# Second attention with block transposes on VectorE, a round trip of the probabilities through DRAM, and modulation accumulated in PSUM

## The reference, cut to what matters

```python
def diff_attend(q, k, v, lam):
    s = jnp.einsum('bqhcd,bkhcd->bchqk', q, k).astype(jnp.float32) * (ATT_HEAD_DIM ** -0.5)
    p = jax.nn.softmax(s, axis=-1)
    a = p[:, 0] - lam * p[:, 1]
    return jnp.einsum('bhqk,bkhe->bqhe', a.astype(v.dtype), v)
...
    for l in range(DEPTH_2):
        mod_l = [m[:, None, :] for m in jnp.split(c_act @ ada_w[l] + ada_b[l], N_MOD, axis=-1)]
        mod_c = jnp.split(cc_act @ ada_w[l] + ada_b[l], N_MOD, axis=-1)
```

## Time and profile before

| | us |
|---|---|
| median of 3 runs | 3024.77 (3024.72 to 3024.81) |
| span of the profiled execution | 3023.4 |
| what lies around the span (median less span) | 1.4 |
| second attention of la = 0, first scores to first work behind the barrier | 865.61 to 1009.97: 144.4 |
| second attention of la = 1, the same | 2259.71 to 2331.57: 71.9 |

### The profile page before, as it was taken

One profiled execution on the slowest core, in us unless ns is written; L12 is line 12 of the kernel. 1 busy time (PEld: TensorE's weight loads), 2 busy tenths in 40 slices (PEclk: granted clock), 3 DMA queues, 4 the chain that ended last, 5 costly groups with the idle time before them and its releaser, 6 DMA issues.

```text
span 3023.4 us, 38857 instructions
## 1 busy us (share of the span) xinstructions
PE 2960.7 (98%) x15464; PEld 2267.7 (75%) x15464; DVE 1376.5 (46%) x2609; ACT 802.6 (27%) x1751; POOL 869.7 (29%) x772
## 2 busy tenths in 40 slices
PE   8999999999999999999999999999998999999999
PEld 7776799998855545555558788888886666678998
DVE  1243267812265736555543533342236555541651
ACT  1022222201022325555620110110104355540210
POOL 0000234574400101221234334443230111110786
PEclk9999999999999999999999999999999999999999
DMA  7455434442345132223212122222331323234443
GB/s 258 151 202 210 147 140 164 157 168 84 126 181 221 44 112 99 84 98 108 88 70 84 70 84 86 96 84 84 112 112 42 116 102 112 105 112 153 154 168 112
DMA packets 65561, 370.18 MB, mean 122 GB/s; under 512 B 6298, under 2 KB 21722, under 8 KB 23152
## 3 DMA queue, kind: packets, MB, share of 16 engines
q1 hardware_dynamic: 49120, 334.60, 30.6%
q10 hardware_dynamic: 15296, 29.56, 2.9%
q0 software_dynamic: 976, 3.63, 0.3%
HBM read 362.30 MB, written 1.28 MB: 120 GB/s over the span
## 4 chain that ended last, share of the span: by engine, by line
PE 89%; DVE 6%; PEld 2%; ACT 1%; issue 1%; PEldq 0%; POOL 0%; DMA 0%; POOLq 0%; SPq 0%; DVEq 0%; ACTq 0%
PE PB L482 15%; PE PB L1361 13%; PE PA L482 11%; PE PS L482 8%; PE PB L362 8%; PE PB L1342 6%; PE PB L1076 5%; PE PB L1192 4%; PE PB L1375 3%; PE PB L406 2%; PE PA L1444 2%; PE PA L1413 1%; PE PA L1427 1%; DVE work L2607 1%; PE PB L1245 1%
## 5 line engine op out<-in xcount | busy, mean ns | idle before, releaser
L1361 PE MATMUL PB<-H,ring 128*128 128x512 f32 (+1 forms) x1024 | 428.1, 566 | 0.0
L1361 PEld LDWEIGHTS PB<-H,ring 128*128 128x128 f32 x1024 | 192.0, 190 | 184.4 <-issue 179.0
L517 POOL TENSOR_TENSOR sums<-ring 128x512 f32<-128x512 f32 x115 | 151.0, 1313 | 617.5 <-PE PA L482 247.5
L482 PE MATMUL PB<-work,sums 128*128 128x128 f32 (+1 forms) x1360 | 230.6, 327 | 0.0
L482 PEld LDWEIGHTS PB<-work,sums 128*128 128x128 f32 x1360 | 207.1, 191 | 17.4
L2861 POOL TENSOR_TENSOR work<-work 128x256 f32<-128x256 f32 x96 | 59.7, 642 | 519.0 <-ACT work L1867 417.0
L482 PE MATMUL PA<-work,sums 128*128 128x128 f32 (+1 forms) x1280 | 208.9, 318 | 0.0
L482 PEld LDWEIGHTS PA<-work,sums 128*128 128x128 f32 x1280 | 187.5, 191 | 13.5
L2521 DVE SCALAR_TENSOR_TENSOR work<-PB,par,work 128x510 f32<-128x510 f32 (+3 forms) x256 | 181.7, 713 | 24.1 <-ACT work L1845 17.3
L626 DVE TENSOR_TENSOR work<-PA,work 128x128 f32<-128x128 f32 (+1 forms) x53 | 18.9, 357 | 379.9 <-ACT work L610 379.9
L1342 PE MATMUL PB<-H,ring 128*128 128x512 f32 (+1 forms) x512 | 175.5, 493 | 0.0
(11 more groups left out here) (394 smaller groups left out, 5305.1 us busy)
## 6 DMA issues: line engine op xcount, KB each, us to landing
ring<-stream SPq DMA_DIRECT2D x314, 1024.0 KB, 4.8
sums<-cs_rows ACTq DMA_DIRECT2D x16, 1024.0 KB, 4.7
sums<-cs_rows ACTq DMA_DIRECT2D x16, 512.0 KB, 3.8
work<-work ACTq DMA_DIRECT2D x16, 256.0 KB, 4.5
work<-scratch POOLq DMA_DIRECT2D x1, 2560.0 KB, 13.5
X<-xT SPq DMA_DIRECT2D x2, 512.0 KB, 5.5
ring<-stream SPq DMA_DIRECT2D x2, 512.0 KB, 6.8
X<-xT SPq DMA_DIRECT2D x1, 1024.0 KB, 20.0
```

Source lines behind the costliest of these rows:

```text
L482: mm = pe.matmul(fast_bank(side, bank)[:, col:col + width], weight(k), right(4 * part + k), start=first and opens and k == 0, stop=last an ...
L517: nc.gpsimd.tensor_tensor(su[:, 0], a21, a22, ALU.add).then_inc(sem("w_summed"), 1)
L1361: mm = pe.matmul(PB[:, pair, t, 0:Tc], ring[:, c % SLOTS, k, t * P:(t + 1) * P], H[:, k, 0:Tc], start=(k == 0), stop=(k == KT - 1))
```

## The change

- `turn2` and `turned2` are gone. In their place DVE's 32 x 32 block transpose (`flip2`, L2487) writes the turned blocks of two units (the two query tiles of one head) into one of three buffers AT_F. SP stores that pair to DRAM (`store_turned`, one DMA of 128 rows, 4 KB each for 512 keys and 2 KB for 256) and fetches it back (`fetch_turned`, four DMAs of 32 partitions, runs of 1 KB or 512 bytes), which puts the 32-row groups where the full transpose wants them, into one of four buffers AT_T.
- `values2(n)` now takes a pair of units, with 256 queries as the moving side, and writes PA[0] only. It stands at step 2n + 7 of the loop (`BEHIND` = 6): one transfer round trip behind. `out2` copies a pair at once.
- The modulation chunks of `ada1` are accumulated in PA[1] over 12 chunks, as those of `ada0` are; DVE's per-chunk adds are gone, one copy per 12 chunks is left.
- The fills move: gates at 8, 23 and 33 (la = 0, of 32 units) and 3, 9 and 17 (la = 1, of 16 units), so that the last one lies behind the last scores; the modulation chunks at the units with u % 4 != 3, over all 32 units.
- SP's loop is split: inside the second attention it is written out, step by step, with stores and fetches among the chunk loads.
- Some semaphores of the residual sums are merged, with the same order.

```diff
-    units, gated = (32, (12, 20, 28)) if la == 0 else (16, (1, 6, 11))
+    units, gated = (32, (8, 23, 33)) if la == 0 else (16, (3, 9, 17))
+    modulated = [u for u in range(units) if u % 4 != 3] if la == 0 else []
...
-        AT_P = [area(L_TMP + at_, 2, TT) for at_ in (0, 1024, 4608)]
-        AT_T = [area(L_TMP + 2048 + 512 * i, 4, P) for i in range(2)]
+        AT_P = [area(L_TMP + 1024 * i, 2, TT) for i in range(3)]
+        AT_F = [area(L_TMP + 3072 + 1024 * i, 2 * TT) for i in range(3)]
+        AT_T = [area(12288 + 1024 * i, 2 * TT) for i in range(4)]
...
+            def store_turned(la, n):
+                nk = units2(la)[2 * n][3]
+                sp.wait_ge(sem("w_flip"), LAYER["w_flip"] * la + 2 * n + 2)
+                sp.dma_start(turned[n % 4, :, 0:2 * nk], AT_F[n % 3][:, 0:2 * nk]).then_inc(sem("turned_out"), 16)
+            def fetch_turned(la, n):
+                nk = units2(la)[2 * n][3]
+                sp.wait_ge(sem("turned_out"), 16 * (LAYER["w_out"] * la + n + 1))
+                if n >= 4:
+                    sp.wait_ge(sem("w_out"), LAYER["w_out"] * la + n - 3)
+                to = AT_T[n % 4][:, 0:2 * nk].rearrange("p (i c) -> p i c", i=4)
+                for g in range(4):
+                    sp.dma_start(to[32 * g:32 * g + 32],
+                                 turned[n % 4, :, nk // 2 * g:nk // 2 * (g + 1)].rearrange("(i q) c -> q i c", i=4))                        .then_inc(turned_in[n % 4], 16)
...
+                for u in range(n_units + 3):
+                    if u >= 3:
+                        n, late = divmod(u - 3, 2)
+                        (fetch_turned if late else store_turned)(la, n)
+                    for _ in fill[u]:
+                        load(c + SLOTS)
+                        c += 1
...
-                def turn2(u):
...
-                def values2(u):
-                    h, qt, k0, nk = us[u]
-                    n = nk // P
-                    pe.wait_ge(sem("w_turned"), LAYER["w_turned"] * la + u + 1)
-                    for i in range(n):
-                        mm = pe.matmul(PA[u % 2][:, 0:P], LV[:, k0 // P + i, h * P:(h + 1) * P],
-                                       AT_T[u % 2][:, i, :], start=(i == 0), stop=(i == n - 1))
+                def values2(n):
+                    h, qt, k0, nk = us[2 * n]
+                    pe.wait_ge(turned_in[n % 4], turned_count(la, n))
+                    if n:
+                        pe.wait_ge(sem("w_out_read"), LAYER["w_out_read"] * la + n)
+                    got = AT_T[n % 4][:, 0:2 * nk].rearrange("p (m t b) -> p t m b", m=8, b=32)
+                    to = PA[0][:, 0:T1].rearrange("p (q i b) -> p i q b", q=2, i=4)
+                    for i in range(nk // P):
+                        mm = pe.matmul(to, LV[:, k0 // P + i, h * P:(h + 1) * P], got[:, i],
+                                       start=(i == 0), stop=(i == nk // P - 1))
                     mm.then_inc(sem("w_out"), 1)
...
+                for u in range(len(us) + BEHIND):
                     if u < len(us):
                         scores2(u)
+                    beside(fill[u], T, 0)
+                    beside(fill[u], T, 1)
+                    if u > BEHIND and u % 2 == 1:
+                        values2((u - BEHIND) // 2)
...
-                def turned2(u):
+                def flip2(u):
                     h, qt, k0, nk = us[u]
+                    v.wait_ge(sem("w_probs"), LAYER["w_probs"] * la + u + 1)
+                    n, t = u // 2, nk // P
+                    if n >= 3 and u % 2 == 0:
+                        v.wait_ge(sem("turned_out"), 16 * (LAYER["w_out"] * la + n - 2))
+                    to = AT_F[n % 3][:, 0:2 * nk].rearrange("p (g q t b) -> p q g t b", g=4, q=2, t=t)[:, u % 2]
+                    vec.transpose(to, AT_P[u % 3][:, 0, 0:nk].rearrange("p (t g b) -> p g t b", g=4, t=t))\
+                        .then_inc(sem("w_flip"), 1)
```

182 lines of the change are left out of this document (77 added, 105 removed).

## The result

The changed kernel takes **3070.07 us** (median of 4, 3054.74 to 3070.47), the kernel before it 3024.74 on the same chip: ratio 1.0128, 95% interval [1.0109, 1.0147]. It is slower by about 1.3%; the prediction said 3020.3, range 3012 to 3033. One of the four executions took 3054.74, and the ratio of the medians is 1.0150. Timed again beside the experiments, the kernel before took either some 3024.4 us, at a mean granted clock of 0.997, or some 3033.7, at 0.993, about equally often (a few lie between), and the experiments' ratios are taken over both groups: against the medians of the lower group alone they are 0.0007 to 0.0022 higher.

What follows compares the result with a forecast made beforehand. It took PE and DVE as both full in the first layer's second attention, DVE as pacing the second's. Span 3023.4 - 5.1 (first) + 0.6 (second) = 3018.9, with 1.4 around it 3020.3 us; range 3012 to 3033.

Steps and rivals of the forecast that it cites:

- PE's clock: PE's granted clock in and behind both second attentions: the sum charged no loss; a fall appeared only as rival D.
- The transpose, DVE's unit: Both second attentions, 512 keys: block transpose 0.72 us long, DVE's whole work per unit 3.49 us.
- rival C: Block transpose on DVE is dear, 1.2 us per 512 columns, making DVE's unit 4.04: total 3031 us; chance 0.04.
- Values of a pair: PE's values matmuls for two query tiles in the second attentions: 1.8 us a pair, 0.9 with 256 keys.
- First attention if nothing waits: First layer's second attention with no wait for transfers: 131.7 us, 12.7 less than before.
- The transfers: First layer's second attention: waits for pairs' store and fetch add 5.9 and 1.7 us, giving 139.3.
- Rival B: SP's chain of store, landing, fetch and load sets the pace, 9.1 then 7.9 us a pair: 3034.0; chance 0.19.
- Second attention: Second layer's second attention, paced by DVE, with the round trip at its end: 72.5 us, 0.6 more than before.
- rival D: PE's clock falls inside the second layer's second attention, matmuls at half rate: some 6 us more, 3026; chance 0.05.

Runs made afterwards that it cites:

- x_no_transfers: The changed kernel without stores and fetches, block transposes writing the values' buffers directly, 32-row groups left in the wrong place: 3019.19 us, ratio 0.9964.
- x_pool_queue: The changed kernel with all stores and fetches issued by GpSimd, chunk loads alone on SP: 3065.51 us, ratio 1.0129.
- y_wide_fetch: The changed kernel fetching each pair with one DMA of 128 rows instead of four of 32 partitions, blocks in wrong order: 3042.55 us, ratio 1.0053.
- x_warm: The changed kernel with matmuls that compute nothing added on PE in both second attentions, in steps where it waits: 3048.85 us, ratio 1.0072.
- y_nt_adds: The changed kernel without stores and fetches, and with the additions per modulation chunk back on DVE: 3029.5 us, ratio 1.0.
- z_accum: The kernel before with only the modulation chunks' accumulation in PSUM, gate chunks moved to units 0, 13 and 28: 3029.72 us, ratio 1.0011.
- v_accum_warm1: z_accum with one matmul that computes nothing in each of the last four steps of the first second attention: 3022.15 us, ratio 0.9981.
- z_tail: The kernel before with only its gate chunks at later units, the last behind the last scores: 3024.09 us, ratio 0.999.

## Why the prediction was wrong

The sum had 3018.9 us of span, the trace 3068.5: 49.6 us too low, and the sign of the change was wrong. Two terms failed above all: the chain of a pair's transfers (7.6 us for 27.7), and PE's clock behind the stages, which the sum put at nothing and which is 17.1. By its own steps:

- **The transpose, DVE's unit** (0.72, 3.49): measured 0.71 and 3.43. Right; rival C falls.
- **Values of a pair** (1.8): 1.92 to 1.99. Right.
- **First attention if nothing waits** (131.7): 138.8 in x_no_transfers, 7.1 too low. Two waits, 3.45 and 2.43 us in x_no_transfers, are PE's second modulation step (L1089) for DVE's copy of the sum (L2185), which stands in DVE's order behind its units. I had priced the accumulation's saving and not its copy. Behind the first wait a pair's values took 3.76 us instead of 1.99, behind the second a gate chunk 15.9 instead of 14.0, at the lower clock.
- **The transfers** (5.9 + 1.7 = 7.6): 27.7. This is the step that failed most. I took a pair's chain as 2.5 MB in 8.0 us in the mean, loads at 2.6 per MB, the rate of a stretch that held nothing but loads, a store as 1.3 and its landing 0.7 behind that, fetches at 2.0, and the start-up of a fetch alike for one DMA or four. Measured, SP's rounds are 10.9 us, a store beside full loads lands in 8.0 us, and issuing one fetch takes 1.74. So the values waited at pairs 3 to 7, 11, 12 and 15, and not at 6, 7 and 12 alone. Rival B named this mechanism (SP's chain) and the pair time from which it decides, 8.8 us, but was priced at 9.1 and had 0.19; its first attention, 152.0, is still 14.5 too short. (The 2.0 us that it quotes stand on their page for DMAs that GpSimd issues; here SP does.) What made the chain long is in the main the loads beside it: cutting their bytes took 23.0 us off and brought the store's landing to 3.2. That it is their bytes and not their place on SP is shown as far as x_pool_queue goes; rate and landing are not told apart.
  The Trainium skill, "DMA: Bandwidth & Descriptors", section "Latency and other measured facts", says that a DMA's fixed cost grows with the load on HBM and is smaller when that is light. The trace goes the same way, 8.0 against 3.2 us for the same store, but by 4.8 us, which includes its time behind the loads. The prediction had taken its fixed part, 1.5 us, from the earlier trace rows as if the load did not matter.
- **Second attention** (72.5): 78.1. Without transfers it is 72.1, with the wide fetch 71.7. So DVE's units were right, and the end of the round trip was too: in y_wide_fetch the last values begin 69.2 us in, for 70.3 in the sum. The rest is PE's clock. Of the 6.0 us between x_no_transfers and the changed kernel 1.4 are in place by the third gate chunk, with the clock at 0.83 in the first 7.3 us, ahead of any fetch; 2.8 are the wait for the last fetch (3.3 for 0.6); and 1.8 are the last values, 3.78 us for 1.97.
- **PE's clock** (rival D, 0.05, 6 us; nothing in the sum): I looked for it inside the second attention alone, in matmuls at half rate. It is 17.1 us behind the two barriers, where PE is busy nearly all the time and has nothing to wait for, and some 5 inside (x_warm). That the transfers bring it is shown by x_no_transfers (1.00 behind both), that it is the clock by x_warm. Which idle time opens it is not: the last values of the second attention, in x_pool_queue, y_wide_fetch and the changed kernel, are

```profile
2356.52 3.41 PE L1333 MATMUL PA<-work 128*128 128x256 f32 x8 [7.75 <-DMA work<-turned]
```

```profile
2346.72 1.99 PE L1352 MATMUL PA<-work 128*128 128x256 f32 x8 [3.19 <-DMA work<-turned]
```

```profile
2363.30 3.78 PE L1355 MATMUL PA<-work 128*128 128x256 f32 x8 [3.34 <-DMA work<-turned]
```

and behind them the clock is 1.00, 1.00 and 0.80. Behind the longest wait it was low for most of these values and then full again, behind 3.19 us it did not fall, behind 3.34 it stayed low into the next stage.

Together 27.2 in the first attention (7.1 + 20.1), 5.6 in the second, 17.1 behind: 49.9 against 49.6, less 0.3 at the start. x_no_transfers and y_nt_adds hold the same work in the second attention and take 72.1 and 69.1 us there: in the first the fifth pair's values ran in 3.78 us at the lower clock, right ahead of the last gate chunk, in the second in 1.99. What stays open is why the clock falls in the one place and not in the other. Nor was it tried to move the chunk loads of the first attention to another stage.

## What to carry to other kernels

Before sending work through DMA to relieve an engine, write down the whole round on the queue that issues it: each issue, each landing, and each load in between. Take the landings from a stretch with that mix, not from the purest one: here 1 MB a pair more, beside loads that had the queues 56% busy, cost 27.7 us, and one store landed in 8.0 us and not in 3.2. Give the consumer one more step: if only the wait moves to the other transfers and the end stays, the round is longer than the consumer's step, and distance won't hide it; whether bytes, landings or issues make it long takes a run of its own for each. And idle time on PE ahead of a barrier can be paid behind it, in a stage that the change doesn't touch; look there in the windows' clock column first.

## What the runs showed of the hardware that I had not expected

- The granted clock fell behind waits of no more than 1.20 and 0.46 us in z_accum's last steps, and the same waits left it at 1.00 in the profiled execution of the kernel before; the 64 matmuls behind took 13.92 or 7.36 us. With four matmuls that compute nothing, 0.43 to 0.46 us each, it stayed at 1.00 in the profiled execution, and all 11 times of v_accum_warm1 lie within 4.7 us. All 10 times of z_tail lie within 3.9 us as well, without such matmuls, with half a gate chunk (7.0 us of PE's work) among the last steps. The kernel before shows 3024 and 3034 us; the lower mean clock of the longer ones, 0.993 for 0.997, says that they lose clock, not where.
- A 0.5 MB store lands in 8.0 us beside 1 MB loads and in 3.2 beside 0.25 MB ones. SP takes 1.74 us to issue a fetch as four DMAs and 0.35 as one; with the one, whose rows are also wider, a stage with full loads is 11.0 us shorter and one with light loads 1.7.
